# Turned rows and small arrays moved to other homes, two weight loads issued earlier, row numbers behind the first up, in a hybrid decoder layer with a mixture of experts

## The chip, the core and the metric

The kernel runs on one core of a Trainium2 chip. The metric is the device time of one execution in microseconds (us): 802.27 us is the median of three runs of the kernel before (802.21 to 802.62). The profile is one further execution of the same program.

## What is computed

One layer of a decoder for 256 prompt tokens and 8 sample tokens, all float32, D_MODEL 1024. A mixer (one input projection, a convolution branch, a recurrent branch with 8 heads, an output projection) is followed by a mixture of experts: each token chooses one of 4 groups and in it the two best of 8 experts, so 2 of 32 experts in all.

```python
def _hier_moe(h, w_router_group, w_router_expert, w_expert_gate, w_expert_up, w_expert_down):
    gp = softmax(ht @ w_router_group); gidx = argmax(gp)
    el = (ht @ w_router_expert) of the chosen group
    tv, ti = lax.top_k(softmax(el), 2)
    ...
    for e in range(N_EXPERTS):
        a = silu(ht @ w_expert_gate[e]) * (ht @ w_expert_up[e])
        out = out + combine[:, e:e + 1] * (a @ w_expert_down[e])
```

A last RMSNorm gives the outputs. The weights of the experts are 32 x 3 matrices of 2 MB each, and every one is read once.

## The kernel before, in words

Each engine has its own instruction stream, and semaphores order them. TensorE (PE) does the matmuls, VectorE (DVE) and ScalarE (ACT) the elementwise work, GpSimd (POOL) some copies and the indirect DMAs, SyncE (SP) issues nearly all loads, in program order, on one DMA queue.

**The stream of expert weights.** The experts are done in 16 pairs, p = 0 to 15. A pair has 12 halves of 1 MB: 4 of gate, 4 of up, 4 of down. `RING` has 20 homes for halves (`NR = 20`), taken from buffers that the mixer has finished with. Half i goes to home i modulo 20. From half 20 on a load waits in `reclaim` (L549) until PE has read what lay in the home before: `m_gate`, `m_up` and `m_down` count quarters of a pair's gate, up and down. From half 24 on most loads take two halves at once (`load_slot`, L567, 2 MB); the two halves of down of pair 2 (32 and 33) take the home of halves 12 and 13, so they wait until all of pair 1's gate is done. Their successors 34 and 35 wait for the same.

**Homes at issue.** Half 17 (up of pair 1) lies in `gates`, over `gaf[0:1984]`; there the small arrays of the choice (`flat`, `small`, L217 to 226) lie before. Half 19 (up of pair 1) lies over `early[0:2048]`; there lie the first two of the three tiles of turned token rows, `xrow`, that ACT writes and that the first gather and the store to `tok_rows` in HBM read. So SP issues half 19 only after the first gather (`m_gathered` 2) and half 17 after `smalls_done`.

**PE's order in the first pairs** (`first_block` and the loop, at the end of the tensor block): output projection with the router, the turning of the rows, ranks of the tokens, gather of block 0 by matmul (L2004), then for pair 0: `gate(0)` (L2040), `row_numbers()` (L2014), `up(0)` (L2040), `turn(0)` (L2067), `down(0)` (L2078), `gather(1)` (L2027); for pair 1: `combine_prompt(0)` (L2086), `gate(1)`, `up(1)` and so on. `row_numbers` computes which token rows stand in the later blocks. DVE copies them to `list_at` (L1497, `list_ready`), POOL then clears a part of `xall` (L785) and issues `fetch_rows(1)` (L781), an indirect DMA of 128 rows of 4 KB from `tok_rows`. `gather(1)` waits for those rows (`row_in`), turns them on PE; DVE scales them (L1462), POOL copies the pair's columns (L796, `m_xe`), and `gate(1)` needs that.

**SP's order there:** halves 10 to 15 behind the chunks of the output projection; half 16; half 18; store of the rows; store of `quad`; half 19; half 17; half 20; the broadcast load of `rows_buf`; halves 21, 22, 23; then slots.

Of the kernel before, what the change touches and what calls it, by code (L numbers as in the profile page):

```python
# [24 lines left out]
P = 128  # L25
D = 1024
KT = D // P
SEQ = 256
NB = 8
T = SEQ + NB  # L30
# [12 lines left out]
SLOTS = 64  # L43
# [9 lines left out]
GATHER = (GATE, UP)  # L53
KEEP = SLOTS
QUART, PART = 32, D // 4
HALF = SLOT // 2
# [35 lines left out]
def hybrid_layer(nc, ins, outs):  # L92
    with ExitStack() as ctx:
# [95 lines left out]
        STORED = {0: (0, 1), 1: (1, 1), 2: (0, 2), 3: (0, 3)}  # L189
        PAIR_ORDER = (1, 0, 2, 3)  # L190

        xrow = early[:, 0:3 * D].rearrange("p (t d) -> p t d", t=3)
        xrow_by = early[:, 0:3 * D].rearrange("p (t a q) -> p t a q", t=3, a=KT)
        xall = early[:, 3 * D:3 * D + KT * COLS].rearrange("p (a c) -> p a c", a=KT)
        act = early[:, 3 * D + KT * COLS:3 * D + KT * COLS + FF]
        assert 3 * D + KT * COLS + FF <= 4 * HT - 128
# [4 lines left out]
        x_samples = vec[:, 0:KT * NB].rearrange("p (a b) -> p a b", a=KT)  # L201
        kept = early[:, 4 * HT - 128:4 * HT]
        row0, sel0 = xall[:, 0, P:2 * P], xall[:, 5:8, P:2 * P]
        row1, sel1 = xall[:, 1, P:LISTED], xall[:, 2:5, P:LISTED]
        hflat = hT[:, :, :].rearrange("p a t -> p (a t)")
        xe = hflat[:, 0:KT * P].rearrange("p (a c) -> p a c", a=KT)
        ytok = hflat[:, KT * P:KT * P + D]
        rows = rows_buf[:, :].rearrange("p (t k) -> p k t", k=4)
        part, both = rows_buf[:, 3 * T:4 * T], rows_buf[:, 3 * T - NG - NE:3 * T]
        PART_AT = (slice(0, NG + NE), slice(64, 64 + NG + NE))  # L210
# [3 lines left out]
        wc = dflat[:, 0:T]  # L214
        wc_samples = dflat[:, SEQ:SEQ + QUART]
        wc_zero = dflat[:, T:T + QUART]
        o = 0  # L217

        def flat(n):
            nonlocal o  # L220
            o += n
            assert o <= HALF
            return gaf[:, o - n:o]

        def small(n):
            return flat(3 * n).rearrange("p (a n) -> p a n", a=3)
# [232 lines left out]
        def _(sp):  # L459
# [7 lines left out]
            def load(c):  # L467
                src, _ = stream[c]
                if c >= STREAM:

                    sp.wait_ge(proj.ready, proj.written(stream[c - STREAM][1]))
                dst = down3(c % STREAM) if c == CO else slot3(c % STREAM)
                sp.dma_start(dst, src).then_inc(stream_in[c % STREAM], 16)
# [112 lines left out]
            sp.wait_ge(o_ready, HEADS)  # L586
            load_slot(4)
            load(WO + 1)

            for n, c in ((5, HO + 1), (6, WO), (7, WO + 1)):  # L590
                assert RING[2 * n][0] == c % STREAM
# [2 lines left out]
                if n == 5:  # L594
                    sp.dma_start(g_by, ins["norm_ffn_g"][0].rearrange("(p a) -> p a", p=P)).then_inc(g_by_in, 16)
            load_half(16)
            sp.wait_ge(misc.ready, misc.written(("ht", 5)))
            sp.wait_ge(x_kept, 1)
            load_half(18)
            sp.wait_ge(row_made, 6)  # L600
            sp.dma_start(tok_rows[0:SEQ, :].rearrange("(t p) d -> p t d", p=P), xrow[:, 0:2, :]).then_inc(rows_kept, 16)
            sp.wait_ge(*misc.read(("ht", 5)))
            sp.dma_start(tok_rows[SEQ:T, :], xrow[0:NB, 2, :]).then_inc(rows_kept, 16)
            sp.wait_ge(quad_ready, 1)
            sp.dma_start(tok_quad[0:SEQ, :].rearrange("(a p) k -> p a k", p=P), quad[:, 0:2, :]).then_inc(quad_kept, 16)
            sp.dma_start(tok_quad[SEQ:T, :], quad[0:NB, 2, :]).then_inc(quad_kept, 16)
            sp.wait_ge(rows_kept, 32)
            sp.wait_ge(m_gathered, 2)
            load_half(19)
            sp.wait_ge(smalls_done, 1)  # L610
            load_half(17)
            load_half(NR)
            sp.wait_ge(quad_kept, 32)
            sp.dma_start(rows_buf[:, :], tok_quad[:, :].rearrange("t k -> (t k)").partition_broadcast(P)).then_inc(rows_ready, 16)
            load_half(NR + 1)
# [50 lines left out]
        def _(pool):  # L666
# [111 lines left out]
            def fetch_rows(b):  # L778
                m = BLOCKS[b][1]
                pool.wait_ge(m_gathered, 2 * b)  # L780
                pool.indirect_dma_start(xrow[0:m, 2, :], None, tok_rows[:, :],  # L781
                                        bass.IndirectOffsetOnAxis(ap=list_at[0:m, b:b + 1], axis=0)).then_inc(row_in, 16)

            pool.wait_ge(m_numbers, 1)
            pool.memset(xall[:, :, LISTED:COLS], 0.0).then_inc(c_const, 1)  # L785
            pool.wait_ge(*made("xend"))
            pool.wait_ge(rows_kept, 32)
            pool.wait_ge(list_ready, 1)
            fetch_rows(1)
            pool.wait_ge(offs_ready, 1)  # L790
# [38 lines left out]
        def _(se):  # L829
# [201 lines left out]
            for i in range(4):  # L1031
                t, half = i // 2, i % 2
                se.wait_ge(y_seated, i + 1)
                se.activation(xrow_by[:, t, :, SLOTS * half:SLOTS * half + SLOTS],
                              bank[Y_BANKS[t][half]][:, :].rearrange("p (q a) -> p a q", a=KT), ACT.Copy,
                              scale=rs[:, t:t + 1]).then_inc(row_made, 1)
            for half in range(2):
                se.wait_ge(misc.ready, misc.written(("ht", 4 + half)))
                se.activation(xrow_by[0:NB, 2, :, SLOTS * half:SLOTS * half + SLOTS],
                              bank[misc.bank(("ht", 4 + half))][0:NB, :].rearrange("p (q a) -> p a q", a=KT), ACT.Copy,  # L1040
                              scale=rs[0:NB, 2:3]).then_inc(M_act, 1)

# [7 lines left out]
            def pair(p):  # L1050
                se.wait_ge(m_gate, 4 * p + 4)
                if p:
                    se.wait_ge(m_turned, p)
                se.activation(act.rearrange("s (f c) -> s c f", f=FT), bank[GATE][:, :].rearrange("s (c f) -> s c f", f=FT),  # L1054
                              ACT.Silu).then_inc(m_silu, 1)
                se.wait_ge(m_turned, p + 1)
                if p:
                    se.wait_ge(m_down, 4 * p)
                se.copy(actT, bank[4][:, :].rearrange("p (f s) -> p f s", f=FT)).then_inc(m_actT, 1)  # L1059
                if p < PAIRS - 1:  # L1060
                    se.wait_ge(m_down, 4 * p + 4)
                else:
                    se.wait_ge(y_lo_in, 1)
                if p:
                    se.wait_ge(m_comb, p)
                    se.wait_ge(m_rows, p)
                for i in range(2) if p < PAIRS - 1 else range(1):
                    se.copy(ytok[:, 512 * i:512 * (i + 1)], bank[4 + i][:, :]).then_inc(m_ytok, 1)  # L1068
# [46 lines left out]
        def _(dve):  # L1115
# [376 lines left out]
            for t, (_, m) in enumerate(TOK_TILES):  # L1492
                step(dve.tensor_scalar(sel1[0:m, t, :], row1[0:m, :], quad[0:m, t, 0:1], None, ALU.is_equal))
                dve.scalar_tensor_tensor(sel1[0:m, t, :], row1[0:m, :], quad[0:m, t, 1:2], sel1[0:m, t, :],
                                         ALU.is_equal, ALU.add).then_inc(m_later, 1)
            dve.wait_ge(m_numbers, 1)
            dve.tensor_copy(list_at[:, 1:], numbers).then_inc(list_ready, 1)  # L1497
            def swiglu(p):
                dve.wait_ge(m_silu, p + 1)
                dve.wait_ge(m_up, 4 * p + 4)  # L1500
# [22 lines left out]

            for p in range(PAIRS):
                swiglu(p)
                if p:
                    add_samples(p - 1)
                weigh(p)
                if p + 1 < len(BLOCKS):
                    for j in range(2):  # L1530
                        gathered(p + 1, j)
# [48 lines left out]
        def _(pe):  # L1580
# [414 lines left out]
            def first_block():  # L1995
                pe.wait_ge(exp_in, 1)
                stay_warm(4, 5)
                pe.wait_ge(row_made, 6)
                pe.wait_ge(*misc.read(("ht", 5)))
                for j in range(2):  # L2000
                    for t, (_, m) in enumerate(TOK_TILES):
                        pe.wait_ge(m_sel, t + 1)
                        for c in range(4):
                            last = mm(bank[GATHER[j]][:, c * P:(c + 1) * P], xrow_by[0:m, t, 4 * j + c, :], sel0[0:m, t, :],  # L2004
                                      start=(t == 0 and c == 0), stop=(t == 2 and c == 3))
                    last.then_inc(m_gathered, 1)

# [10 lines left out]
            def gather(b):  # L2018
                n = BLOCKS[b][1]
                pe.wait_ge(row_in, 16 * b)  # L2020
                if b > 1:
                    pe.wait_ge(m_added, b - 1)
                else:
                    pe.wait_ge(m_act, 1)
                for j in range(2):
                    for c in range(4):
                        last = tr(bank[GATHER[j]][:, c * n:(c + 1) * n], xrow_by[0:n, 2, 4 * j + c, :], ident[0:n, 0:n])  # L2027
                    last.then_inc(m_gathered, 1)

            def hidden(p, kind, out, done, between=None):  # L2030
# [23 lines left out]
            def up(p):  # L2054
                pe.wait_ge(m_xall, 2 * min(p, len(BLOCKS) - 1) + 2)
                if p:
                    pe.wait_ge(m_act, p)
                hidden(p, 1, bank[UP], m_up)

            def turn(p):  # L2060
                pe.wait_ge(m_act, p + 1)
                if p:
                    pe.wait_ge(m_ytok, 2 * p)
                else:
                    pe.wait_ge(smalls_done, 1)
                for f in range(FT):
                    last = tr(bank[4][:, f * P:(f + 1) * P], act[:, f * P:(f + 1) * P], ident[:, :])  # L2067
                last.then_inc(m_turned, 1)
# [47 lines left out]
            for p in range(PAIRS):  # L2116
                if p == 1:
                    combine_prompt(p - 1)
                gate(p)
                if p == 0:  # L2120
                    row_numbers()
                if 1 < p < PAIRS - 1:
                    combine_prompt(p - 1, 2 if late_rows(p - 1) else 4)
                up(p)
                if p:
                    combine_samples(p - 1)
                if p and late_rows(p - 1):
# [100 lines left out]
```

## Time and profile before

| | us |
|---|---|
| median of three runs | 802.27 |
| profiled execution, own time | 801.55 |
| its span | 799.8 |
| PE busy in the span | 776.8 (97%) |
| DVE, ACT, POOL busy | 236.5, 172.6, 96.6 |
| DMA moved | 266.82 MB |

The page divides the span into 40 slices; PE shows nine tenths or more in nearly all of them. The DMA line shows nine tenths or more from the eighteenth slice (340 us) to the last but one, where the experts run. The granted clock line shows nine or more throughout. The chain that ended last is 76% PE and 19% DMA. Busy PE is not PE at its peak, and an engine that waits in the middle of its stream makes everything behind it wait. A DMA row gives the time from issue to landing; of a load in an empty queue that is the transfer and its overhead, and what is above it is time behind other loads.

### The profile page before, as it was taken

To read this page: it belongs to the slowest core of one execution; us is meant where nothing else is said; L and a number is where in the kernel's file an instruction comes from. 1 tells how busy PE (TensorE), PEld (TensorE's weight loads), DVE (VectorE), ACT (ScalarE), POOL (GpSimd) and SP (SyncE) were. 2 spreads that over 40 slices of the span, in tenths; PEclk is the share of its full clock that TensorE was granted. 3 is DMA by queue.
4 is the path that set the end of the run, shared out by engine and by line. 5 is a ranking of instruction groups with operands and counts; after the bars stand their busy time and mean duration, and the time that the engine had idled before them with its cause. 6 is when DMAs were issued, how large, how long until landed. Compare 5 with 4: busy or idle time off the path is not lost.

```text
span 799.8 us, 10083 instructions
## 1 busy us (share of the span) xinstructions
PE 776.8 (97%) x4132; PEld 440.1 (55%) x4132; DVE 236.5 (30%) x540; ACT 172.6 (22%) x313; POOL 96.6 (12%) x130
## 2 busy tenths in 40 slices
PE   8999999999999999999999999999998999999996
PEld 7888888888888887853333333333323333323332
DVE  4099859482550321441201110011101101101102
ACT  3104333657544101410011001110010010011101
POOL 5200064523300000001101000001000000000001
PEclk9999999999999999999999999999999999999999
DMA  9845586668749975589999999999999999999994
GB/s 331 246 153 187 164 236 201 187 211 183 264 147 360 399 265 206 188 325 433 423 429 416 427 429 428 429 425 429 427 426 429 429 427 427 429 426 420 421 410 156
DMA packets 76374, 266.82 MB, mean 334 GB/s; under 512 B 5726, under 2 KB 37706, under 8 KB 63775
## 3 DMA queue, kind: packets, MB, share of 16 engines
q1 hardware_dynamic: 74402, 263.05, 84.4%
q10 hardware_dynamic: 1461, 1.45, 0.6%
q0 software_dynamic: 464, 1.64, 0.5%
q8 instruction: 35, 0.57, 0.3%
q14 instruction: 12, 0.10, 0.0%
HBM read 259.14 MB, written 7.47 MB: 333 GB/s over the span
## 4 chain that ended last, share of the span: by engine, by line
PE 76%; DMA 19%; DVE 1%; issue 1%; POOL 1%; SPq 0%; ACT 0%; DVEq 0%
PE bank L1642 23%; PE bank L2040 22%; DMA slots<-in_w_expert_gate_dram 10%; PE bank L2078 8%; PE bank L1915 7%; PE bank L2086 5%; DMA x_early<-in_w_expert_gate_dram 5%; DMA slot<-in_w_expert_up_dram 3%; PE bank L1862 2%; PE bank L1752 1%; DMA slots<-in_w_in_dram 1%; PE bank L2004 1%; PE bank L1674 1%; PE bank L2067 1%; PE bank L2092 1%
## 5 line engine op out<-in xcount | busy, mean ns | idle before, releaser
L1642 PE MATMUL bank<-hT,slots 128*128 128x264 f32 x832 | 189.6, 387 | 0.0
L2040 PE MATMUL bank<-slots,hT 128*64 128x512 f32 x624 | 181.8, 601 | 5.6 <-DMA slots<-in_w_expert_gate_dram 5.0
L1642 PEld LDWEIGHTS bank<-hT,slots 128*128 128x128 f32 x832 | 156.6, 190 | 26.8 <-issue 0.6
L2040 PEld LDWEIGHTS bank<-slots,hT 128*64 128x64 f32 x624 | 55.8, 138 | 107.3 <-issue 94.2
L1501 DVE TENSOR_TENSOR x_early<-x_early,bank 128x512 f32<-128x512 f32 x16 | 11.0, 688 | 344.5 <-PE bank L2040 344.5
L2078 PE MATMUL bank<-slots,wrep 128*64 128x512 f32 x304 | 85.1, 595 | 0.1
L2040 PE MATMUL bank<-slot,hT 128*64 128x512 f32 x208 | 81.9, 595 | 2.4 <-DMA slot<-in_w_expert_gate_dram 1.7
L2086 PE MATMUL bank<-hT,diag 128*128 128x512 f32 x128 | 64.4, 615 | 0.2 <-ACT hT L1068 0.2
L796 POOL COPY hT<-x_early 128x512 f32 x30 | 17.6, 614 | 369.5 <-PE bank L2040 285.5
L2078 PEld LDWEIGHTS bank<-slots,wrep 128*64 128x64 f32 x304 | 26.1, 137 | 45.6 <-issue 40.1
L1226 DVE SCALAR_TENSOR_TENSOR slot<-slot,rows_buf 128x256 f32<-128x256 f32 x120 | 49.4, 488 | 0.0
L1059 ACT COPY wrep<-bank 128x512 f32<-128x512 f32 x16 | 9.4, 586 | 164.9 <-PE bank L2067 164.9
L2040 PE MATMUL bank<-x_early,hT 128*64 128x512 f32 x96 | 42.3, 594 | 1.7 <-DMA x_early<-in_w_expert_gate_dram 1.7
L2078 PE MATMUL bank<-slot,wrep 128*64 128x512 f32 x112 | 42.7, 596 | 0.7 <-ACT wrep L1059 0.7
L2040 PE MATMUL bank<-gates,hT 128*64 128x512 f32 x96 | 42.5, 594 | 0.0
L1068 ACT COPY hT<-bank 128x512 f32<-128x512 f32 x31 | 16.7, 589 | 116.6 <-PE bank L2078 116.6
L1054 ACT ACTIVATE x_early<-bank 128x512 f32<-128x512 f32 x16 | 16.9, 1057 | 114.7 <-PE bank L2040 114.7
L2040 PEld LDWEIGHTS bank<-slot,hT 128*64 128x64 f32 x208 | 24.5, 137 | 30.2 <-issue 25.1
L2086 PEld LDWEIGHTS bank<-hT,diag 128*128 128x128 f32 x128 | 21.0, 189 | 29.1 <-issue 28.6
L1915 PE MATMUL bank<-gates,slots 128*128 128x264 f32 x128 | 29.4, 388 | 0.0
L1915 PE MATMUL bank<-x_early,slots 128*128 128x264 f32 x128 | 28.6, 386 | 0.0
L1915 PEld LDWEIGHTS bank<-gates,slots 128*128 128x128 f32 x128 | 24.1, 190 | 5.2 <-DVE x_early L1404 1.3
(313 smaller groups left out, 747.7 us busy)
## 6 DMA issues: line engine op xcount, KB each, us to landing
slots<-in_w_expert_gate_dram SPq DMA_DIRECT2D x15, 2048.0 KB, 26.3
slots<-in_w_expert_up_dram SPq DMA_DIRECT2D x15, 2048.0 KB, 31.2
slots<-in_w_expert_down_dram SPq DMA_DIRECT2D x15, 2048.0 KB, 33.6
slots<-in_w_in_dram SPq DMA_DIRECT2D x13, 2048.0 KB, 10.2
slots<-in_w_expert_gate_dram SPq DMA_DIRECT2D x10, 1024.0 KB, 26.4
slot<-in_w_expert_gate_dram SPq DMA_DIRECT2D x5, 2048.0 KB, 25.4
slot<-in_w_expert_up_dram SPq DMA_DIRECT2D x5, 2048.0 KB, 26.2
slot<-in_w_expert_down_dram SPq DMA_DIRECT2D x5, 2048.0 KB, 29.5
```

The costliest lines, as they stand in the source:

```text
L796: pool.tensor_copy(xe[:, :, e * SLOTS:(e + 1) * SLOTS], xall[:, :, bass.ds(at[e], SLOTS)]).then_inc(m_xe, 1)
L1054: se.activation(act.rearrange("s (f c) -> s c f", f=FT), bank[GATE][:, :].rearrange("s (c f) -> s c f", f=FT), ACT.Silu).then_inc(m_silu, 1)
L1059: se.copy(actT, bank[4][:, :].rearrange("p (f s) -> p f s", f=FT)).then_inc(m_actT, 1)
L1068: se.copy(ytok[:, 512 * i:512 * (i + 1)], bank[4 + i][:, :]).then_inc(m_ytok, 1)
L1226: i = dve.scalar_tensor_tensor(conv[:, c, 0:SEQ], upad[:, c, j:j + SEQ], taps[:, c, j:j + 1], conv[:, c, 0:SEQ], ALU.mult, ALU.add)
L1501: dve.tensor_tensor(act.rearrange("s (f c) -> s f c", f=FT), act.rearrange("s (f c) -> s f c", f=FT), bank[UP][:, :].rearrange("s (c f) -> ...
L1642: last = mm(out, w[:, a, t * P:(t + 1) * P], (hT if c else xgain)[:, a, :], start=(a == 0), stop=(a == KT - 1))
L1862: last = mm(bank[proj.bank(("ya", d))][:, 0:T], w[:, c, d * P:(d + 1) * P], conv[:, c, :], start=(c == 0), stop=(c == CT - 1))
L1915: last = mm(bank[proj.bank((label, d))][:, 0:T], w[:, a, (d % 4) * P:(d % 4 + 1) * P], src[:, a, :], start=(a == 0), stop=(a == KT - 1))
L2040: last = mm(out[sl, :], xe[:, a, sl], expert_view(p, kind, e, a // 2)[:, a % 2, :], start=(a == 0), stop=(a == KT - 1))
L2078: last = mm(bank[4 + i][sl, :], actT[:, f, sl], expert_view(p, 2, e, f)[:, 0, 512 * i:512 * i + 512], start=(f == 0), stop=(f == FT - 1))
L2086: return mm(bank[Y_BANKS[t][i]][:, :], wc[:, t * P:(t + 1) * P], ytok[:, CHUNK * i:CHUNK * (i + 1)], start=False, stop=stop, skip_group_ch ...
```

## The change

It has five parts.

1. The three tiles of turned rows are no longer together in `early[0:3*D]`: tile 0 goes to `ytok`, tile 1 to `rows_buf[:, 0:D]`, tile 2 stays. The store to `tok_rows` becomes three DMAs, the first after the first two activations; who waits for the store waits for 48. ACT, before it first writes `ytok`, waits for the store too, and the load of `rows_buf` stands behind it on SP.
2. The small arrays of the choice lie in `act` and in columns of `xall`.
3. Half 19 is issued right behind the last chunk of the output projection; half 17 behind half 16, after DVE's last sum of squares (`f_sum` 7). `load_half(NR)` (half 20) now stands ahead of the wait for the rows' store.
4. `row_numbers()` stands behind `up(0)` and no longer ahead of it.
5. DVE copies the row numbers behind `swiglu(0)`, and `turn(0)` waits for `list_ready` in place of `smalls_done`, since it overwrites the bank with the numbers.

```diff
-        xrow = early[:, 0:3 * D].rearrange("p (t d) -> p t d", t=3)
+        small_homes = [act, *(xall[:, a, 2 * P:LISTED] for a in (0, 5, 6, 7))]
+        xrow = [ytok, rows_buf[:, 0:D], early[:, 2 * D:3 * D]]
...
             load_slot(4)
             load(WO + 1)
+            load_half(NR - 1)
...
             load_half(16)
+            sp.wait_ge(f_sum, KT - 1)
+            load_half(17)
             sp.wait_ge(misc.ready, misc.written(("ht", 5)))
             sp.wait_ge(x_kept, 1)
             load_half(18)
-            sp.wait_ge(row_made, 6)
-            sp.dma_start(tok_rows[0:SEQ, :].rearrange("(t p) d -> p t d", p=P), xrow[:, 0:2, :]).then_inc(rows_kept, 16)
+            for t in range(2):
+                sp.wait_ge(row_made, 2 * t + 4)
+                sp.dma_start(tok_rows[t * P:(t + 1) * P, :], xrow[t]).then_inc(rows_kept, 16)
...
-            sp.wait_ge(rows_kept, 32)
+            load_half(NR)
+            sp.wait_ge(rows_kept, 48)
             sp.wait_ge(m_gathered, 2)
-            load_half(19)
-            sp.wait_ge(smalls_done, 1)
-            load_half(17)
-            load_half(NR)
             sp.wait_ge(quad_kept, 32)
             sp.dma_start(rows_buf[:, :], ...)
             load_half(NR + 1)
@@ ACT, pair(p), ahead of the copies to ytok
+                if p == 0:
+                    se.wait_ge(rows_kept, 48)
@@ DVE
-            dve.wait_ge(m_numbers, 1)
-            dve.tensor_copy(list_at[:, 1:], numbers).then_inc(list_ready, 1)
...
             for p in range(PAIRS):
                 swiglu(p)
+                if p == 0:
+                    dve.wait_ge(m_numbers, 1)
+                    dve.tensor_copy(list_at[:, 1:], numbers).then_inc(list_ready, 1)
@@ PE, turn(0)
-                    pe.wait_ge(smalls_done, 1)
+                    pe.wait_ge(list_ready, 1)
@@ PE, the loop over pairs
                 gate(p)
-                if p == 0:
-                    row_numbers()
...
                 up(p)
+                if p == 0:
+                    row_numbers()
```

## Rows read from the trace of the kernel before

**Rows 1.** Windows: PE, PEld, DVE, ACT, POOL busy (x count), clock, DMA share, GB/s.

```profile
320.00:330.00 10.00, 10.00 (x52) 7.94 (x50) 2.32 (x6) 1.82 (x5) 0.31 (x1) 1.00 0.01 3
344.00:348.00 4.00, 4.00 (x24) 2.03 (x25) 3.05 (x12) 1.94 (x3) 0.00 (x0) 1.00 0.41 107
...
600.00:700.00 100.00, 95.42 (x404) 33.08 (x402) 11.47 (x20) 8.73 (x13) 4.70 (x8) 0.98 1.01 428
700.00:785.00 85.00, 82.14 (x354) 27.35 (x352) 8.59 (x15) 8.17 (x12) 2.35 (x4) 1.00 1.00 414
```

**Rows 2.** Waits of PE, 340 to 800: total, times, longest us.

```profile
PE bank L2040 <- DMA slots<-in_w_expert_gate_dram: 5.0, 4, 2.0
...
PE bank L2040 <- DMA x_early<-in_w_expert_gate_dram: 1.7, 1, 1.7
```

**Rows 3.** Chain that ended last, in order of time: start, us, what; one load.

```profile
548.37 39.34 DMA slots<-in_w_expert_gate_dram
```

**Rows 4.** The same chain, 345 to 385 us: PE's work in pairs 0 and 1.

```profile
345.28 7.02 PE bank L2040 x32
352.30 3.56 PE bank L2014 x24
355.85 7.04 PE bank L2040 x32
...
363.73 0.67 PE bank L2067 x4
...
365.06 7.11 PE bank L2078 x32
...
373.41 3.67 PE bank L2086 x8
377.08 8.30 PE bank L2040 x37
```

**Rows 5.** Timeline of SP's issues, 313 to 392 us: start, us, what.

```profile
329.56 0.43 SPq L562 DMA_DIRECT2D gates<-in_w_expert_up_dram  x1
...
346.07 0.35 SPq L562 DMA_DIRECT2D x_early<-in_w_expert_up_dram  x1
347.09 0.35 SPq L562 DMA_DIRECT2D gates<-in_w_expert_up_dram  x1
...
348.90 3.76 SPq L562 DMA_DIRECT2D slots<-in_w_expert_down_dram  x3
...
384.19 0.80 SPq L572 DMA_DIRECT2D slots<-in_w_expert_down_dram  x2
```

**Rows 6.** DMA issues by window: from issue to landing, us; issued 313.41, 384.19, 391.06.

```profile
slots<-in_w_expert_gate_dram SPq DMA_DIRECT2D x1, 2048.0 KB, 7.8
...
slots<-in_w_expert_down_dram SPq DMA_DIRECT2D x1, 2048.0 KB, 9.4
...
gates<-in_w_expert_gate_dram SPq DMA_DIRECT2D x1, 2048.0 KB, 12.8
```

**Rows 7.** Timeline of POOL, 350 to 380 us: what leads to the first fetch.

```profile
355.92 0.53 POOL L785 MEMSET x_early<- 128x512 f32 x1 [22.03 <-PE bank L2014]
357.02 1.22 POOL L781 DMA_INDIRECT x_early<-tok_rows,list_at  x1 [0.58 <-POOL x_early L785]
```

**Rows 8.** DMA issues: the fetches issued at 357.02, 375.57 and 397 us.

```profile
x_early<-tok_rows,list_at POOLq DMA_INDIRECT x1, 9.0
...
x_early<-tok_rows,list_at POOLq DMA_INDIRECT x1, 11.9
...
x_early<-tok_rows,list_at POOLq DMA_INDIRECT x1, 10.9
```

**Rows 9.** DMA packets by queue while fetch 1, then fetch 2 moved (361.3:365.3, 379.7:386.4).

```profile
q1 hardware_dynamic: 160, 1.18, 69.8%
...
q1 hardware_dynamic: 161, 2.34, 82.9%
```

**Rows 10.** Timeline of all engines, 363 to 395 us: gather(1).

```profile
372.08 1.09 PE L2027 MATMUL bank<-ident,x_early 128*128 128x128 f32 x8
```

**Rows 11.** Timeline of PE from 613 us, and the window behind that wait.

```profile
617.43 8.78 PE L2040 MATMUL bank<-slots,hT 128*64 128x512 f32 x30 [2.02 <-DMA slots<-in_w_expert_gate_dram]
...
618.70:622.10 3.40, 3.40 (x10) 0.96 (x8) 0.00 (x0) 0.00 (x0) 0.00 (x0) 0.50 1.05 448
```

More of the change, by code:

```diff
@@ L190, in hybrid_layer @@
         PAIR_ORDER = (1, 0, 2, 3)
-        xrow = early[:, 0:3 * D].rearrange("p (t d) -> p t d", t=3)
-        xrow_by = early[:, 0:3 * D].rearrange("p (t a q) -> p t a q", t=3, a=KT)
         xall = early[:, 3 * D:3 * D + KT * COLS].rearrange("p (a c) -> p a c", a=KT)
@@ L207, in hybrid_layer @@
         ytok = hflat[:, KT * P:KT * P + D]
+        xrow = [ytok, rows_buf[:, 0:D], early[:, 2 * D:3 * D]]
+        xrow_by = [x.rearrange("p (a q) -> p a q", a=KT) for x in xrow]
         rows = rows_buf[:, :].rearrange("p (t k) -> p k t", k=4)
@@ L216, in hybrid_layer @@
         wc_zero = dflat[:, T:T + QUART]
-        o = 0
+        taken = [0] * len(small_homes)
         def flat(n):
[L220 to L223, printed above, removed]
+            i = next(i for i, home in enumerate(small_homes) if taken[i] + n <= home.shape[1])
+            taken[i] += n
+            return small_homes[i][:, taken[i] - n:taken[i]]
         def small(n):
@@ L599, in _ @@
             load_half(18)
-            sp.wait_ge(row_made, 6)
-            sp.dma_start(tok_rows[0:SEQ, :].rearrange("(t p) d -> p t d", p=P), xrow[:, 0:2, :]).then_inc(rows_kept, 16)
+            for t in range(2):
+                sp.wait_ge(row_made, 2 * t + 4)
+                sp.dma_start(tok_rows[t * P:(t + 1) * P, :], xrow[t]).then_inc(rows_kept, 16)
             sp.wait_ge(*misc.read(("ht", 5)))
-            sp.dma_start(tok_rows[SEQ:T, :], xrow[0:NB, 2, :]).then_inc(rows_kept, 16)
+            sp.dma_start(tok_rows[SEQ:T, :], xrow[2][0:NB, :]).then_inc(rows_kept, 16)
             sp.wait_ge(quad_ready, 1)
@@ L780, in fetch_rows @@
                 pool.wait_ge(m_gathered, 2 * b)
-                pool.indirect_dma_start(xrow[0:m, 2, :], None, tok_rows[:, :],
+                pool.indirect_dma_start(xrow[2][0:m, :], None, tok_rows[:, :],
                                         bass.IndirectOffsetOnAxis(ap=list_at[0:m, b:b + 1], axis=0)).then_inc(row_in, 16)
@@ L786, in _ @@
             pool.wait_ge(*made("xend"))
-            pool.wait_ge(rows_kept, 32)
+            pool.wait_ge(rows_kept, 48)
             pool.wait_ge(list_ready, 1)
@@ L1033, in _ @@
                 se.wait_ge(y_seated, i + 1)
-                se.activation(xrow_by[:, t, :, SLOTS * half:SLOTS * half + SLOTS],
+                se.activation(xrow_by[t][:, :, SLOTS * half:SLOTS * half + SLOTS],
                               bank[Y_BANKS[t][half]][:, :].rearrange("p (q a) -> p a q", a=KT), ACT.Copy,
@@ L1038, in _ @@
                 se.wait_ge(misc.ready, misc.written(("ht", 4 + half)))
-                se.activation(xrow_by[0:NB, 2, :, SLOTS * half:SLOTS * half + SLOTS],
+                se.activation(xrow_by[2][0:NB, :, SLOTS * half:SLOTS * half + SLOTS],
                               bank[misc.bank(("ht", 4 + half))][0:NB, :].rearrange("p (q a) -> p a q", a=KT), ACT.Copy,
@@ L2003, in first_block @@
                         for c in range(4):
-                            last = mm(bank[GATHER[j]][:, c * P:(c + 1) * P], xrow_by[0:m, t, 4 * j + c, :], sel0[0:m, t, :],
+                            last = mm(bank[GATHER[j]][:, c * P:(c + 1) * P], xrow_by[t][0:m, 4 * j + c, :], sel0[0:m, t, :],
                                       start=(t == 0 and c == 0), stop=(t == 2 and c == 3))
@@ L2026, in gather @@
                     for c in range(4):
-                        last = tr(bank[GATHER[j]][:, c * n:(c + 1) * n], xrow_by[0:n, 2, 4 * j + c, :], ident[0:n, 0:n])
+                        last = tr(bank[GATHER[j]][:, c * n:(c + 1) * n], xrow_by[2][0:n, 4 * j + c, :], ident[0:n, 0:n])
                     last.then_inc(m_gathered, 1)
```

## The prediction, made before the changed kernel was run

> **What bounds the kernel now.** I read the windows first. From 348 us on the DMA queue is full: in the last 185 us its share is 1.00 to 1.01 at 414 to 428 GB/s, while PE has idle time [rows 1]. Then the waits: in the experts PE waits for weights, 5.0 and 1.7 us by two of its lines, 2.0 us the longest [rows 2]. The chain says the same: a load issued at 548.37 us needs 39.34 us to land [rows 3], against 7.8 us in an empty queue [rows 6], so some 30 us of other loads lie ahead of it. The end of the kernel is therefore set by this: the last moment at which the queue had nothing to move, plus the bytes behind it at a fixed rate. A saving counts only if it lies ahead of that moment, and a hole in the queue later than that costs all its length.
>
> Where is that moment? In 320 to 330 us the queue is empty (share 0.01) and in 344 to 348 us it is 0.41 busy [rows 1]; then it stays full, but barely. The proof is the first load that waits for pair 1's gate (half 32): issued at 384.19 us [rows 5] it lands after 9.4 us, and 7.8 us is what a 2 MB load takes in an empty queue [rows 6]. The queue had only 9.4 - 7.8 = 1.6 us of work too much. The next pair of loads, at 391.06 us, has 12.8 - 7.8 = 5.0 us [rows 6], and PE is faster per pair than the loads, so the surplus grows from there. So half 32 is the neck: whatever is prefetched ahead of it gains at most 1.6 us, unless PE's path to the end of gate(1) also gets shorter; and what lengthens that path by more than 1.6 us makes the kernel slower.
>
> **Part 3, the early loads.** A half is 1.05 MB, at 428 GB/s [rows 1] 2.45 us, two are 4.9 us. Half 19 moves from 346.07 us [rows 5] to the time behind the output projection's last chunk. The queue is empty again in 320 to 330 us [rows 1], so this load finds room and delays nothing that PE needs; it costs 0.4 us of SP's time. If that cover were gone, the next halves would come 2.45 us later, and they are not used before 345 us. Half 17 moves from 347.09 us to behind half 16 (329.56 us) [rows 5]; SP waits there for f_sum, which DVE gives before the turned rows for which SP waits next anyway, so half 18 is not late. The stores of the rows come behind one more half, 2.45 us later, some 348 us instead of 345. Behind SP's wait for them stand the load of rows_buf and half 21, which waits for PE until 348.90 us anyway [rows 5]; I take nothing, at most 1 us on loads that are not the neck. The others who wait for the store are the fetch (364 us) and ACT's first copy to ytok (372 us): nothing. Half 20 can't move, it waits for PE's first quarter of gate(0). So up to the neck the queue has 4.9 us less to do, and 1.6 us of it can be gained.
>
> **Parts 1 and 2, other homes.** The same instructions with the same shapes on ACT, DVE and PE; two more 0.4 us issues on SP. Start of gate(0) stays at 345.28 us [rows 4]. Cost between -0.2 and +0.3 us; I take 0.
>
> **Parts 4 and 5, row numbers behind up(0).** All from [rows 4]. gate(0) ends at 352.30. up(0) takes 7.04 and ends at 359.34 in place of 362.89; that frees its quarters 3.5 us sooner, which fills the queue that part 3 has emptied (without it the queue would run dry near 357 us). row_numbers takes 3.56: 359.34 + 3.56 = 362.90. It covers DVE's product after up, which before left PE idle until turn(0) at 363.73. Now turn(0) waits for DVE's small copy behind the numbers, some 0.2 us: it starts at 363.1, which is 0.6 us sooner, and down(0) ends at 372.17 - 0.6 = 371.6. So far a gain of 0.6 us.
>
> But the fetch hangs on the row numbers. Before, they ended at 355.85, and POOL issued the fetch at 357.02 [rows 7], 1.17 us later. Now: 362.90 + 1.17 = 364.07. The first fetch landed after 9.0 us, at 366.0, and gather(1) began only at 372.08 [rows 10], so it had 6.1 us to spare; it loses 7.05 us of them and down(0) comes 0.6 us sooner: PE waits at least 7.05 + 0.6 - 6.1 = 1.6 us. It will be more. The fetches behind it took 11.9 and 10.9 us [rows 8]. The reason is in the packets: while fetch 1 moved, 160 packets of queue 1 brought 1.18 MB, while fetch 2 moved, 161 packets brought 2.34 MB [rows 9], packets twice as large, since by then 2 MB loads are under way. With two halves gone from the queue, the 2 MB loads (issued from 356 us on) are what moves when the fetch moves now, at 368 to 374 us. I take 11.4, the middle of the two later rows: landing at 375.5, between 373.1 (by 9.0) and 376.0 (by 11.9). PE waits from 371.6 to 375.5, 3.9 us. On PE combine_prompt(0) and gate(1) stand behind this wait. From gather(1)'s start to gate(1)'s was 377.08 - 372.08 = 5.0, of which 0.2 was a wait for ACT that is over by now: gate(1) starts at 375.5 + 4.8 = 380.3, which is 3.2 us later than before (0.8 by the low end, 3.7 by the high end). POOL's copy for pair 1 needs 3.3 us from the gather's start, so it stays hidden.
>
> **The clock.** PE waited 2.02 us until 617.43, and right behind it a window shows a granted clock of 0.50, 1.2 GHz, for 3.4 us; behind the wait of 1.7 us [rows 2], which lies in the window from 700 us, it stays at 1.00 [rows 1, 11]. A wait of 3.9 us is twice the first. I take it that the clock falls: 3.4 us at half speed do the work of 1.7, so gate(1) ends another 1.7 us later. The Trainium skill has the rule ("TensorE: Matmul & The Clock Gate", Part 1: The HAM clock gate): the array's clock is halved when PE has been idle lately and given back once it is busy. By that rule the trace agrees.
>
> **The sum.** gate(1) ends 3.2 + 1.7 = 4.9 us later, and half 32 is issued at 384.19 + 4.9 = 389.1. The queue is dry by then (its earlier work lasted to 393.6 - 4.9 = 388.7 before, and 4.9 us of it are gone), so it lands 7.8 later at 396.9; before, 384.19 + 9.4 = 393.6. All behind it moves by +3.3 us, and nothing later takes it back, since the queue stays full: the following pair of loads had 5.0 us to spare and keeps 3.4. Against the profiled execution's own time 801.55 + 3.3 = 804.9; that execution lies 0.7 us under the median of the runs, and from the median 802.27 + 3.3 = 805.6. I forecast the latter.
>
> **Rivals.**
> The clock stays (chance 0.17). The wait is then paid only once: +3.2 - 1.6 = +1.6 us, 803.9. For it: most of PE's waits in the experts left the clock alone. Against it: all of them were under 2.02 us.
> The fetch is as quick as the first (0.10). Landing at 373.1, a wait of 1.6 us, no fall of the clock, gate(1) 0.8 us later, -0.8 us in all: 801.5. It decides if the queue has a hole at 368 us; by my count the loads issued at about 356 and 359.4 last until 370, and the next is issued at 368.2.
> The prefetch pays in full (0.15), the other side: the queue isn't dry at half 32, because transfers here run slower than I count or because PE's wait is hidden. Then the two halves bring 4.9 us at the most, 797.4, and 1.6 + 0.6 = 2.2 us (800.1) if only the fetch lands before 371.6. For the latter the fetch would have to take under 7.5 us, which no fetch of 128 rows does [rows 8]. The Trainium skill's rule speaks for this rival ("DMA: Bandwidth & Descriptors", Rules for kernel authors): issue a DMA early and wait for it late. The trace agrees for the weights and disagrees for the fetch, which this change issues later.
> More is lost (0.10): two slow stretches of the clock, or a fetch beyond 12 us: +5 us, 807.3.
> Of the queues the Trainium skill says ("DMA: Bandwidth & Descriptors", Queues, rings and completion order) that an engine takes turns between them packet by packet, so a fetch beside larger packets is slower. By that rule the trace agrees [rows 9].
>
> **How the numbers follow.** My forecast has 0.48, with a range of its own of 804.4 to 806.6. 0.2% is 1.6 us, about what can be told from no change: under 800.67 is faster, over 803.87 slower. Faster: the full prefetch, 0.15. Same: the quick fetch 0.10 and a good half of the clock rival, 0.10. Slower: the rest, 0.65. The range for 8 in 10 takes the quick fetch, the clock rival, the forecast and the near part of the last one: 801.3 to 807.0.
>
> **What would show it.** In the profile of the changed kernel: up(0) directly behind gate(0) at 352.3, row_numbers from 359.3; the fetch issued at 364.1 and landing after some 11 us; PE idle before L2027, released by the fetch, for 3 to 4 us from about 371.6; the clock at 0.50 for 3.4 us behind it; the DMA share below 0.5 in some window of 381 to 389; half 32 landing 7.8 us after its issue. If L2027 doesn't wait, step 4 is wrong; if half 32 takes more than 9 us to land, the neck is wrong.

## The result, and the profile after

The changed kernel takes 806.0 us (median of six runs, 805.08 to 810.14), the kernel before beside it 802.44 (802.21 to 803.26). The medians differ by 3.6 us. The ratio over all runs on record is 1.0054, with a 95% interval of 1.0043 to 1.0064, that is 3.4 to 5.1 us slower; the two medians alone give 1.0044. On another chip, later (after_again, below), it was 805.55 to 802.42 us, 3.1 us by the medians, ratio 1.0036 (1.0022 to 1.0049).

The profiled execution is the slowest of the six: own time 810.14 us, span 808.3. Its first expert matmul, gate(0), starts at 349.05 us in place of 345.28 [rows 4], 3.77 us late. The two differences lie at the kernel's start, which the change doesn't touch: the first load of the kernel took 9.06 us (6.97 before), and PE's first 16 matmuls behind it, which then had half the clock, 5.51 us (3.83 before). The chain of the kernel after:

```profile
2.46 9.06 DMA slots<-in_w_in_dram
11.52 0.04 issue
11.56 5.51 PE bank L1757 x16
```

and a window of it, with the columns of [rows 1]:

```profile
12.10:15.50 3.40, 3.40 (x9) 2.62 (x8) 0.38 (x1) 0.09 (x1) 2.88 (x12) 0.50 1.05 399
```

The second profile of the same kernel doesn't have it (gate(0) at 345.67). It comes and goes: e3_warm, e4_fetch_free and e9_rows_later below have it too (gate(0) at 347.7 to 348.0), and e6_before_halves and e7_mid_up a late first load alone (346.4 and 346.5). The half clock at the start is in 4 of the 10 profiles of kernels made from the changed one and in none of the 4 with the old homes; that is too few to say that the homes have no part in it. So below, times of one profile are counted from its gate(0). Here is that second profile (after_again, own time 805.75 us, span 804.0), the chain through pairs 0 and 1, the lines that answer to [rows 4]:

```profile
345.67 13.88 PE bank L2045 x64
359.56 3.57 PE bank L2019 x24
...
364.28 11.26 DMA x_early<-tok_rows,list_at
...
375.59 1.61 PE bank L2032 x8
377.20 4.61 PE bank L2091 x8
381.80 13.88 PE bank L2045 x64
```

gate(0) and up(0) are one piece of 64 matmuls now, the row numbers (L2019) follow. Then the chain leaves PE: for 11.26 us it is the fetch. turn(0) and down(0), which lie in that time, are off the chain. The issue of the fetch, in POOL's timeline:

```profile
364.28 1.47 POOL L782 DMA_INDIRECT x_early<-tok_rows,list_at  x1 [0.58 <-POOL x_early L786]
```

and PE's wait, in its own:

```profile
368.25 3.60 PE L2083 MATMUL bank<-slots,wrep 128*64 128x512 f32 x16
375.59 1.61 PE L2032 MATMUL bank<-ident,x_early 128*128 128x128 f32 x8 [3.74 <-DMA x_early<-tok_rows,list_at]
```

Behind the wait of 3.74 us the clock is at 0.50 (1.2 GHz) in the window from 376.0 to 379.4 us, and that is why gather(1) takes 1.61 us and combine_prompt(0) 4.61, in place of 1.09 [rows 10] and 3.67 [rows 4]. And the DMA queue runs dry, between 382 and 390 us: its share (second last column) falls to 0.49 and 0.20.

```profile
372.60:376.00 3.40, 0.41 (x4) 0.41 (x5) 0.00 (x0) 0.37 (x1) 0.00 (x0) 1.00 1.02 430
376.00:379.40 3.40, 3.40 (x10) 2.00 (x9) 1.38 (x2) 0.00 (x0) 1.16 (x2) 0.50 1.02 434
...
382.00:386.00 4.00, 4.00 (x20) 1.30 (x18) 0.00 (x0) 0.00 (x0) 0.00 (x0) 1.00 0.49 197
386.00:390.00 4.00, 4.00 (x22) 1.36 (x20) 0.00 (x0) 1.07 (x1) 0.00 (x0) 1.00 0.20 37
```

It waits for the end of gate(1), which frees the home of half 32: SP issues that load at 388.91 us (before 384.19 [rows 5]), and it lands after 8.1 us. The issue in SP's timeline:

```profile
388.91 0.81 SPq L572 DMA_DIRECT2D slots<-in_w_expert_down_dram  x2
```

In the first profile, of the kernel after, it is issued at 393.20 and lands after 7.8 us, which is the time of an empty queue [rows 6]; from its DMA issues:

```profile
slots<-in_w_expert_down_dram SPq DMA_DIRECT2D x1, 2048.0 KB, 7.8
```

Later both kernels have a full queue: in the kernel after, 1.01 and 427 GB/s from 600 to 700 us, against 1.01 and 428 [rows 1].

### The profile page after: what moved, and what is told of

The parts are those of the page before. It is cut to its first block, busy times and chain, and to the rows that moved or that the text cites. A ratio compares the mean times of both kernels' runs of the same rounds, so it can differ in the third digit from the quotient of the medians.

```text
span 808.3 us, 10085 instructions
## 1 busy us (share of the span) xinstructions
PE 779.5 (96%) x4132; PEld 440.7 (55%) x4132; DVE 240.1 (30%) x540; ACT 172.6 (21%) x313; POOL 97.0 (12%) x130
## 4 chain that ended last, share of the span: by engine, by line
PE 75%; DMA 20%; issue 1%; DVE 1%; POOL 1%; SPq 0%; ACT 0%; DVEq 0%; POOLq 0%
PE bank L1647 23%; PE bank L2045 21%; DMA slots<-in_w_expert_gate_dram 10%; PE bank L2083 7%; PE bank L1920 7%; PE bank L2091 5%; DMA x_early<-in_w_expert_gate_dram 5%; DMA slot<-in_w_expert_up_dram 3%; PE bank L1867 2%; DMA x_early<-tok_rows,list_at 1%; PE bank L1757 1%; DMA slots<-in_w_in_dram 1%; PE bank L2009 1%; PE bank L1679 1%; PE bank L2072 1%
## 5 line engine op out<-in xcount | busy, mean ns | idle before, releaser
L2045 PE MATMUL bank<-slots,hT 128*64 128x512 f32 x624 | 179.0, 595 | 5.4 <-DMA slots<-in_w_expert_gate_dram 5.4
L1647 PEld LDWEIGHTS bank<-hT,slots 128*128 128x128 f32 x832 | 156.6, 190 | 26.8 <-issue 0.6
```

The lines of the kernel that those rows point to most:

```text
L1647: last = mm(out, w[:, a, t * P:(t + 1) * P], (hT if c else xgain)[:, a, :], start=(a == 0), stop=(a == KT - 1))
L2045: last = mm(out[sl, :], xe[:, a, sl], expert_view(p, kind, e, a // 2)[:, a % 2, :], start=(a == 0), stop=(a == KT - 1))
```

## The experiments

The theory: the queue's last dry moment sets the end; half 32 is the neck; the late fetch delays gate(1) and with it half 32. Each kernel was timed beside the kernel before on its own chip, and profiled once. The ratio takes in all the runs and so need not be that of the two medians. A table gathers them; "half 32" is the time from gate(0)'s start to half 32's landing in the profile, against 48.3 us before (384.19 + 9.4 - 345.28 [rows 4 to 6]).

| kernel | median, before beside it (us) | ratio (95%) | half 32, against before |
|---|---|---|---|
| after | 806.0, 802.44 | 1.0054 (1.0043 to 1.0064) | +3.6 |
| after_again | 805.55, 802.42 | 1.0036 (1.0022 to 1.0049) | +3.0 |
| e1_prefetch_only | 801.03, 802.16 | 0.9982 (0.9973 to 0.9992) | -1.3 |
| e2_numbers_only | 805.31, 802.16 | 1.0033 (1.0023 to 1.0044) | +1.3; +4.2 in e2b |
| e3_warm | 806.36, 802.16 | 1.0040 (1.0026 to 1.0055) | +2.0; +1.7 in e3b |
| e4_fetch_free | 801.27, 802.16 | 0.9985 (0.9976 to 0.9994) | -1.4 |
| e5_prefetch_halves | 800.57, 802.49 | 0.9977 (0.9964 to 0.9990) | -2.7 |
| e6_before_halves | 802.22, 802.49 | 0.9994 (0.9982 to 1.0006) | -0.1 |
| e7_mid_up | 801.28, 802.49 | 0.9981 (0.9969 to 0.9993) | -1.4 |
| e9_rows_later | 799.06, 802.49 | 0.9956 (0.9940 to 0.9972) | -3.1 |
| e10_warm5 | 804.39, 802.42 | 1.0026 (1.0012 to 1.0040) | +1.4 |

**e1_prefetch_only.** The changed kernel with the row numbers back ahead of up(0):

```diff
                 gate(p)
+                if p == 0:
+                    row_numbers()
...
                 up(p)
-                if p == 0:
-                    row_numbers()
```

(and DVE's copy ahead of `swiglu`).

> The changed kernel with parts 4 and 5 undone: row_numbers between gate(0) and up(0), DVE's copy ahead of swiglu(0); the early loads of halves 17 and 19 and the new homes stay. My theory (half 32 is the neck, and the late fetch costs all of the loss): L2027 doesn't wait, the clock stays at 1.00, gate(1) ends as before, half 32 lands 7.8 us after its issue in place of 9.4, the queue has a hole before it; time 1.6 us under the kernel before, 800.8 (800.4 to 801.3). Rival A (the prefetch pays in full): 4.9 us under it, 797.5. Rival B (the new homes or the early loads cost time by themselves): 803 to 806.

Measured: 1.1 us under the kernel before by the medians, -0.6 to -2.2 by the interval. PE's path is the old one (gate(1) at 376.96), and half 32, issued at 384.07, lands after 8.1 us and not 9.4. Windows of this kernel show the hole that the two early halves leave ahead of it (0.75), and one behind the stores of the rows (0.89; the kernel before has 0.96 there):

```profile
348.00:352.00 4.00, 4.00 (x20) 1.15 (x16) 1.99 (x5) 0.00 (x0) 0.00 (x0) 1.00 0.89 242
382.00:386.00 4.00, 4.00 (x22) 1.33 (x20) 0.00 (x0) 1.07 (x1) 0.00 (x0) 1.00 0.75 247
```

So the prefetch brings 1.1 us of 4.9 by the medians, 1.3 at half 32, and the new homes cost nothing that can be seen. Both rivals fall.

**e2_numbers_only, e2b_numbers_only.** The kernel before with the row numbers behind up(0), DVE's copy behind swiglu(0) and turn(0)'s wait for it:

```diff
                 gate(p)
-                if p == 0:
-                    row_numbers()
...
                 up(p)
+                if p == 0:
+                    row_numbers()
```

> The kernel before with parts 4 and 5 alone: row_numbers behind up(0), DVE's copy behind swiglu(0), turn(0) waits for it; loads and homes as before. My theory: the fetch is issued at 364, lands some 11 us later, PE waits 3 to 4 us, the clock falls, half 32 is issued 5 us later and is the neck with or without the prefetch: as slow as the changed kernel, +3.3 to +3.7 us, 805.9. Rival (the loss comes from the emptied queue as much as from the fetch): clearly less slow than the changed kernel, +2 us or less.

Measured: +3.15 us by the medians, a little under the +3.3 to +3.7 that were expected, and as much as the changed kernel on the second chip (+3.13). So parts 4 and 5 alone make as large a loss as the whole change, and with them the prefetch brings nothing to be seen. The rival falls. The runs fall in two groups, 803.3 to 804.2 and 805.2 to 806.4 us. The profile was of one of the quick ones (803.96). Its PE waits only 2.2 us for the fetch, because the granted clock fell before, in the window from 364.3 us, and made down(0) longer:

```profile
360.90:364.30 3.40, 2.72 (x20) 1.77 (x18) 1.24 (x3) 0.30 (x1) 0.67 (x2) 1.00 1.01 429
364.30:367.70 3.40, 3.06 (x8) 1.01 (x10) 0.67 (x2) 0.29 (x1) 1.33 (x1) 0.50 1.07 455
...
374.50:377.90 3.40, 2.43 (x12) 1.70 (x13) 1.29 (x2) 0.00 (x0) 0.26 (x1) 1.00 0.97 414
```

That slow stretch lies inside the time that PE would have waited anyway, and behind the fetch the clock is 1.00. A second profile was to show the other group.

> e2_numbers_only for a second profile: its runs fall into 803.3 to 804.2 and 805.2 to 806.4 us. My theory: it is where the clock falls: in the first profile (803.96) it fell at 364.3, ahead of down(0), and the slow stretch lay inside the time in which PE would have waited for the fetch; where it falls behind the wait, gate(1) ends 1.7 us later, 805.5 or more.

Its time was 807.43 us, of which a late gate(0) is 0.75. Here PE waits 3.8 us and the clock is at 0.50 for two stretches behind the wait; gather(1) and combine_prompt(0) take 1.97 and 5.19 us. The chain, and then the windows:

```profile
364.91 11.35 DMA x_early<-tok_rows,list_at
...
376.31 1.97 PE bank L2028 x8
378.27 5.19 PE bank L2087 x8
383.46 13.88 PE bank L2041 x64
```

```profile
374.90:378.30 3.40, 1.99 (x9) 2.00 (x10) 0.69 (x1) 0.00 (x0) 0.00 (x0) 0.50 0.99 420
378.30:381.70 3.40, 3.40 (x5) 1.33 (x5) 0.69 (x1) 0.00 (x0) 2.13 (x3) 0.50 1.02 434
```

In both profiles the fetch lands 29.9 to 30.0 us behind gate(0)'s start. What differs is gather(1) and combine_prompt(0): 1.09 + 3.44 us in the first, 1.97 + 5.19 in the second, 2.6 us more. So where the clock falls makes nearly all of the 2.9 us between the two at half 32 (+1.3 and +4.2). That the timed runs fall in two groups for the same reason is likely but not shown, since only these two were profiled.

**e4_fetch_free.** The changed kernel, but the first fetch doesn't need the numbers:

```diff
+            step(pool.iota(list_at[:, 1:2], pattern=[[0, 1]], base=0, channel_multiplier=1))
+            pool.wait_ge(rows_kept, 48)
+            fetch_rows(1)
             pool.wait_ge(m_numbers, 1)
...
-            fetch_rows(1)
```

(DVE copies the other numbers alone.) This kernel leaves out the right rows: block 1 gets token row 0 in all its 128 places.

> The changed kernel, but the first fetch takes a list of zeros made by GpSimd ahead and is issued once the rows are stored, near 351 us, so it hangs no longer on the row numbers; it fetches token row 0 for block 1, so the outputs of the experts from block 1 are not the reference's. All else, the numbers' place behind up(0) included, stays. My theory: no wait at L2027, down(0) ends 0.6 us sooner than before, half 32 is issued at 383.6 by the clock of the profile before and lands 7.8 us later: 2.2 us under the kernel before, 800.2 (799.6 to 800.8). Rival A (the prefetch pays in full once PE doesn't wait): 797.5. Rival B (the place of the numbers costs by itself): 803 or more.

Measured: 801.27 against 802.16 us, -0.9 (expected -2.2). The wait at the gather is gone, the clock stays at 1.00, and all of the loss is gone, though the numbers stand behind up(0). So the loss comes from when the fetch is issued, and nothing else about that place costs time that can be seen. Counted from gate(0), half 32 is issued 0.7 us sooner than before, as expected, but it took 8.7 us, since now the queue had 0.9 us of work left: it landed 1.4 us sooner, as in e1_prefetch_only. That showed me a second limit close behind the first, the queue itself.

**e7_mid_up.** How long may the fetch be delayed? The prefetch, with the numbers in the middle of up(0):

```diff
-                hidden(p, 1, bank[UP], m_up)
+                hidden(p, 1, bank[UP], m_up, row_numbers if p == 0 else None)
```

> The prefetch alone, with row_numbers in the middle of up(0), that is 3.5 us later than in the kernel before and 3.5 us earlier than in the changed one; DVE's copy ahead of swiglu(0). My theory (the fetch has 6.1 us to spare, less 2 us for its slower landing): the fetch is issued at 360.5, lands near 371.5, L2032 waits 0 to 0.5 us, the clock stays; as e1_prefetch_only within 0.4 us, 801.0. Rival (each us of delay of the numbers costs the same, or the freed quarters of up gain something): 802.5 or more, or 800.2 or less.

Measured: 801.28, -1.2 us. POOL's timeline, the DMA issue and PE's timeline of this kernel:

```profile
361.69 1.22 POOL L782 DMA_INDIRECT x_early<-tok_rows,list_at  x1 [0.58 <-POOL x_early L786]
```

```profile
x_early<-tok_rows,list_at POOLq DMA_INDIRECT x1, 11.4
```

```profile
373.32 1.09 PE L2032 MATMUL bank<-ident,x_early 128*128 128x128 f32 x8
```

The fetch lands at 361.69 + 11.4 = 373.1, gather(1) starts at 373.32 without a wait, 26.8 us behind gate(0) as in the kernel before. 3.5 us of delay use the spare time up to the last 0.2 us and cost nothing; 7 us cost 3.7 to 3.9 us of waiting (2.2 where the clock had fallen ahead of it).

**e6_before_halves, e5_prefetch_halves.** Is half 32's issue the neck? Pair 1's gate by halves of both experts, so that half 32 is issued after half of gate(1):

```diff
-            return p == PAIRS - 2 or (p, kind) in ((1, 2), (PAIRS - 1, 0))
+            return p == PAIRS - 2 or (p, kind) in ((1, 0), (1, 2), (PAIRS - 1, 0))
```

> The kernel before with pair 1's gate loaded by halves, nothing else. My theory: half 32 is issued 3.5 us earlier, but the queue was still 1.6 us full when it was issued before, so it only waits longer in the queue: no change, 802.2 (within 0.4 us). Rival (an earlier half 32 helps by itself): up to 1.6 us faster.

> The prefetch alone (as in e1_prefetch_only), and pair 1's gate loaded by halves of both experts, so that the home of halves 12 and 13 is free after half of gate(1): half 32 is issued 3.5 us earlier, near 380.6. My theory (half 32's issue is the neck): it now lands right behind the load before it, which in e1_prefetch_only left a hole of 1.1 us, so 1.1 us under e1_prefetch_only: 799.9 (799.4 to 800.4). Rival (the neck lies elsewhere, or the 1.6 us are all that the queue had): no change against e1_prefetch_only, 801.0.

Measured: alone it changes nothing (802.22 to 802.49, half 32 at -0.1 us); it waits longer in the queue. With the prefetch -1.9 us by the medians, half 32 lands 1.4 us sooner than in e1_prefetch_only. Half 32 among the DMA issues, issue to landing, of e6:

```profile
slots<-in_w_expert_down_dram SPq DMA_DIRECT2D x1, 2048.0 KB, 12.8
```

and of e5:

```profile
slots<-in_w_expert_down_dram SPq DMA_DIRECT2D x1, 2048.0 KB, 10.1
```

In both it is well above the 7.8 to 8.2 of the dry cases, so the queue was not dry. The halves alone bring nothing; on top of the prefetch they bring 1.4 us at half 32. That is what a neck looks like. But it rests on one profile of each: the time of e5 against e1 (800.57 and 801.03, on two chips, each to its own before: 0.9977 and 0.9982) is no difference beyond the intervals, and 800.57 lies just above the range that was expected.

**e9_rows_later.** In e1's windows half 21 came late: SP stood at the waits for the stores, and the load of rows_buf took it 1.42 us. The edit puts half 21 ahead of both, on top of e5:

```diff
             load_half(NR)
+            load_half(NR + 1)
             sp.wait_ge(rows_kept, 48)
...
-            load_half(NR + 1)
```

> As e5_prefetch_halves, and half 21 issued ahead of the load of rows_buf and of SP's waits for the stores (part 3 put half 21 behind them, where it was issued at 350.1 in place of 348.9 and landed 2.6 us later than the missing bytes alone would have it). My theory: the hole at 353 to 356 shrinks, half 32 lands 3.5 to 4.1 us sooner than in the kernel before: 798.6 (798.0 to 799.4). Rival (only holes at half 32 count, the ones ahead are covered): as e5_prefetch_halves.

Measured: 799.06 against 802.49 us, ratio 0.9956 (0.9940 to 0.9972), 3.4 us faster, the fastest of all versions here. Against e5 on the same chip it is 1.5 us by the medians. In the profile half 32 lands 3.1 us sooner than before (expected 3.5 to 4.1), which is only 0.4 sooner than in e5. So what holds half 21 up between 348 and 352 us costs time once the neck is gone; where the other 1.1 us of it went isn't shown, and the profiled run was the slowest of the eight (801.31, with its gate(0) 2.4 us late).

**e3_warm, e3b_warm, e10_warm5.** Is it the clock that makes the second part of the loss? Matmuls of ones in PE's waiting time:

```diff
                 if p == 0:
+                    pe.wait_ge(m_act, 1)
+                    stay_warm(GATE, 9)
                     gather(1)
```

> The changed kernel, with nine matmuls of ones (128x256, 0.39 us each) on PE between down(0) and gather(1), 3.5 us of work in the time in which PE waits for the fetch; the result of these matmuls is overwritten. My theory: the wait for the fetch shrinks to some 0.4 us, the clock stays at 1.00, gather(1) and combine_prompt(0) take 1.1 and 3.7 us in place of 2.0 and 5.0, gate(1) starts 2 us sooner: 1.7 to 2.2 us under the changed kernel, 804.0. Rival (the clock isn't on the path or falls all the same): no change, 806.0.

Measured: 806.36, no better than the changed kernel. Its profile shows what I expected (clock 1.00, gather(1) 1.09 us; the nine matmuls took 4.15 us, and the wait that is left is 0.29), half 32 at +2.0. The second profile:

> e3_warm for a second profile: its median was 806.4 although its profile showed no fall of the clock and half 32 1.6 us sooner than in the changed kernel. If the clock falls in this one, at turn(0) or in the nine matmuls, the matmuls don't keep it up reliably, and they then delay gather(1); if it stays at 1.00 and the time is 804 or less, the runs of e3_warm had other delays.

It again shows 1.00 throughout the stage, half 32 at +1.7, and a time of 804.39, between the two cases that the expectation named. Six of the seven timed runs lie from 805.6 to 807.1, and no trace of those but the first (807.09, which had a gate(0) 2.65 us late) exists. The mean granted clock of each run is on record: 0.994 or 0.995 in the five without a trace, as in the changed kernel (0.993 to 0.996), and 0.997 in the quick one of 803.65 us. So the clock may have fallen in those five all the same, with the matmuls in place. A mean over the whole run can't say where (the kernel before has 0.993 to 0.998), so what they lost stays open. Five matmuls in place of nine:

> As e3_warm with five matmuls in place of nine, some 2 us of work, so that they don't delay gather(1) where the clock has fallen already at turn(0) (as in the profile of e2_numbers_only, at 364.3 us). My theory: the clock stays at 1.00 behind the fetch, or has fallen once before and the slow stretch ends inside the wait: 1 to 2 us under after_again. Rival (the clock isn't what the rest of the loss is): as after_again within 0.4 us.

Measured: 804.39 (803.79 to 805.02), 1.2 us under after_again on the same chip, though the two intervals of the ratio overlap. The profile has a wait of 1.40 us and the clock at 1.00:

```profile
371.60:375.00 3.40, 2.36 (x11) 1.75 (x10) 0.00 (x0) 1.07 (x2) 0.00 (x0) 1.00 1.03 431
375.00:378.40 3.40, 3.04 (x13) 1.89 (x14) 1.29 (x2) 0.00 (x0) 0.87 (x2) 1.00 1.02 434
```

In this profile and in after_again's the fetch lands 29.9 us behind gate(0), and gate(1) starts 34.5 us behind it here and 36.1 there: the slow stretch costs 1.7 us on PE's path, and half 32 lands 1.7 us sooner here. So the clock is worth 1.7 us in the traces; the timed runs agree in e10 without proving it, and those of e3 speak against it.

**after_again.**

> The changed kernel once more, beside e10_warm5 on one chip, for a second look at its clock and its start. My theory: 3.3 to 4.3 us over the kernel before; L2032 waits some 4 us for the fetch, and the clock falls behind that wait for one or two stretches of 3.4 us; a later start of gate(0), as the first profile had it (3.8 us), is no part of the change and needn't come again. Rival: the late start is part of it, gate(0) starts after 348 us again.

Measured: +3.1 us by the medians, a little under what was expected. Its readings stand in the first section: L2032 waits 3.74 us, the clock falls for one stretch, and the late gate(0) did not come again.

## Why the prediction was right

The forecast was 805.6 us, +3.3 on 802.27; measured were 806.0, +3.6, and +3.1 on the second chip. The mechanism came as forecast: the late fetch, PE's wait for it, the clock, the dry queue at half 32. That the number fits within 0.3 us is in part luck, since terms that were off by 0.3 to 1 us went against each other, as below.

*The neck.* Forecast: a surplus of 1.6 us at half 32, so the prefetch gains no more. Shown by e1 (-1.1 us, half 32 at -1.3) and by e6 (no gain from an earlier issue alone); e5 shows the gain of both together in its profile, not beyond the noise of its times. The full prefetch of 4.9 us, the rival on the other side, fell in e1 and e4. It leaned on issuing early and waiting late, and the prediction says that the trace disagrees with that for the fetch; the trace of the kernel before agrees for the fetch too (issued at 357.02, needed at 372.08), and it is the change that gives this up. The queue is full from 348 us, as the prediction has it, and not from 340: the page's DMA line has eight tenths in the eighteenth slice and nine from the nineteenth, 360 us, on.

*The fetch.* Forecast: issued at 364.07, landing after 11.4, a wait of 3.9 us. Measured 363.9 (less the shift of gate(0)) and 11.3, wait 3.74 in the second profile; 363.9, 11.4 and 3.88 in the first. That a fetch beside 2 MB loads is slower than beside 1 MB loads rested on [rows 8, 9]. In the second profile 164 packets of queue 1 brought 2.42 MB from 368.5 to 375.5 us, the large packets that were expected there, and e7's fetch took 11.4 us beside such packets too. The one in e4, issued at 352.81, took 8.1 us, and from 357 to 361 us 173 packets brought 1.25 MB; but it fetched one row 128 times, so it is no clean comparison. The other side is in the kernel after itself: its second fetch, 128 rows again, was issued at 383.30 us in the first profile and 379.43 in the second, and had the dry stretch ahead of half 32 nearly to itself. It took 6.9 and 6.5 us, against 11.9 in the kernel before, where the queue was full. So how long a fetch takes hangs on what moves beside it; "no fetch of 128 rows" under 7.5 us held for [rows 8] alone. The Trainium skill says that a DMA engine goes from queue to queue a whole packet at a time ("DMA: Bandwidth & Descriptors", Queues, rings and completion order). These times agree with it; no run here changes the size of the packets alone, so the cause isn't shown.

*From the fetch to gate(1).* Forecast: 4.8 us at full clock. Measured 4.53 where the clock stayed (e10): 0.3 too much.

*The clock.* Forecast: one stretch of 3.4 us at half speed, 1.7 us lost. The second profile has just that: 1.61 + 4.61 = 6.22 us for gather(1) and combine_prompt(0), and at full clock (e10) they take 1.09 + 3.44 = 4.53. The first profile has two stretches, and so has e2b, and there the two pieces take 1.97 + 5.02 and 1.97 + 5.19 us: 2.5 to 2.6 us lost. That I had in the rival "more is lost" with 0.10; with two of the four profiles that had no matmuls of ones and a late fetch, it looks too low. And e2's first profile shows a fall that I hadn't thought of, at turn(0), which costs little.

*Half 32.* Forecast: issued at 389.1 and landing after 7.8. Measured, less the shift of gate(0): 388.5 and 389.4; 8.1 and 7.8. It lands 3.0 and 3.6 us later than before, for the forecast's 3.3.

*What I set too low.* "I take nothing, at most 1 us" for SP's waits ahead of half 21: in e1 it was issued at 350.1 and not 348.9, and in after_again at 351.4. In the changed kernel it doesn't count, since half 32 comes later still; without the neck it does, e9. And the sum is a sum at half 32, with nothing for what comes behind it. From half 32's landing to the end of the span the profile of the kernel before has 406.2 us and that of e6 406.0, all the others 406.8 to 407.8; in after_again it is 0.8 us more than before, in the first profile of the kernel after 1.1. In the same way the medians of e1, e4 and e5 fell by 0.2, 0.5 and 0.8 us less than half 32 did. Where that went isn't shown. The forecast had no such term.

*Homes and early issue at no cost.* e1 bears it out within its interval.

## What to carry to other kernels

Where a transfer queue is the bound, look for its last dry moment, and for the load whose time from issue to landing is nearest to that of an empty queue: a prefetch ahead of it gains no more than that load's surplus, and what delays its release costs everything beyond. Before moving a small computation behind a large one, follow what hangs on it through the other engines: here a block of 3.6 us on PE was moved for a gain of 0.6 us, and the fetch that hangs on it, which had 6.1 us to spare, was issued 7 us later and took 2.3 us longer.

## What the runs showed of the hardware

An indirect fetch of 128 rows of 4 KB took 9.0 us beside 1 MB loads (8.7 to 9.6 at the same place in e1, e5, e6 and e9) and 10.9 to 11.9 us beside 2 MB loads (8.1 us in e4, where all 128 were the same row), and 6.5 and 6.9 us with the weight queue nearly dry. A wait of PE of 2.0 us [rows 11] and waits of 3.7 to 3.9 us were followed by a granted clock of 0.50, for 3.4 or 6.8 us; waits of 1.4 (e10) and 2.2 us (e2) were not. It also fell once (e2, at 364.3 us) where PE had only short waits of 0.35 and 0.67 us around turn(0) behind the small matmuls of the row numbers, while in seven other profiles with the same order it stayed.
